# Seven products of half sums in place of eight for part of a decoder's input projection, on one Trainium2 core

## The reference, cut to what matters

```
xn = rmsnorm(x, norm_gain)
h  = xn @ w_in                                   # 1024 -> 5960 columns
cb, cc, cu, cz, q, k, v, az, iq, ik, iw, gc, ga = split_cols(h)
y_conv = cb * short_conv(cc * cu) * silu(cz)                       # width 512
y_attn = sparse attention(q, k, v; top 256 keys by iq, ik, iw) * silu(az)
m = sigmoid(gc) * (y_conv @ w_up_conv) + sigmoid(ga) * (y_attn @ w_up_attn)
x = x + m @ w_out ; y = rmsnorm(x, final_gain)
```

## Time and profile before

| | us |
|---|---|
| median of 3 runs | 2862.32 (2861.93 to 2862.68) |
| profiled execution, own time | 2864.7 |
| its span | 2862.9 |
| prompt tiles, from normalising tile 1 (T = 2) to the end of the stage | 213.8 to 1833.5 |
| sample stage | 1838.9 to 2357.9 |

### The profile page before, as it was taken

One profiled execution on the slowest core, in us unless ns is written; L12 is line 12 of the kernel. 1 busy time (PEld: TensorE's weight loads), 2 busy tenths in 40 slices (PEclk: granted clock), 3 DMA queues, 4 the chain that ended last, 5 costly groups with the idle time before them and its releaser, 6 DMA issues. The chain is left out here.

```text
span 2862.9 us, 31303 instructions
## 1 busy us (share of the span) xinstructions
PE 2663.6 (93%) x11650; PEld 1481.7 (52%) x11650; DVE 1932.3 (67%) x3938; ACT 832.8 (29%) x1363; POOL 49.0 (2%) x65
## 2 busy tenths in 40 slices
PE   7987998999999999999999998899999868999988
PEld 5743444454444545454545454555555546676653
DVE  5219899987797989887989997126995014454443
ACT  4222233322323233333333333311221342231210
POOL 0000000000000000000000000100000100000000
PEclk9998999999999999999999999899999989999999
DMA  7111111111111111111111010131225749453307
GB/s 213 32 37 35 43 42 41 31 46 35 40 45 35 36 38 30 41 38 37 33 35 35 26 43 24 52 115 72 103 104 126 220 193 292 156 187 108 129 30 30
DMA packets 212680, 215.33 MB, mean 75 GB/s; under 512 B 76720, under 2 KB 199216, under 8 KB 208880
## 3 DMA queue, kind: packets, MB, share of 16 engines
q1 hardware_dynamic: 203824, 153.13, 18.6%
q0 software_dynamic: 7072, 60.18, 6.8%
q10 hardware_dynamic: 1632, 0.01, 0.1%
HBM read 157.56 MB, written 55.72 MB: 74 GB/s over the span
## 5 line engine op out<-in xcount | busy, mean ns | idle before, releaser
L787 PE MATMUL attn_ps_r<-xnT,early 128*128 128x424 f32 (+2 forms) x2464 | 993.1, 543 | 30.5 <-ACT early L638 15.7
L115 DVE TENSOR_SCALAR_CACHE_REDUCE early<-early 128x384 uint8<-128x384 f32 (+13 forms) x462 | 681.8, 1476 | 11.5
L787 PEld LDWEIGHTS attn_ps_r<-xnT,early 128*128 128x128 f32 x2464 | 442.9, 191 | 441.0 <-issue 423.5
L1089 PE MATMUL samp_ps_r<-xnT,early 128*128 128x424 f32 (+1 forms) x800 | 288.2, 523 | 6.1 <-PEq L89 6.1
L657 ACT ACTIVATE attn_probT<-attn_ps_p 128x512 f32<-128x512 f32 (+1 forms) x288 | 151.9, 571 | 407.2 <-PE attn_ps_p L832 407.0
L1646 PE MATMUL merge_ps_y<-merge_w_out,merge_merged 128*128 128x512 f32 (+1 forms) x544 | 235.0, 592 | 1.2 <-DVE merge_merged L1775 1.2
L1089 PEld LDWEIGHTS samp_ps_r<-xnT,early 128*128 128x128 f32 x800 | 153.2, 192 | 138.9 <-issue 138.3
L715 DVE SCALAR_TENSOR_TENSOR early<-attn_relu,early 128x512 f32<-128x512 f32 (+3 forms) x266 | 182.1, 684 | 31.4 <-ACT attn_relu L674 4.1
L638 ACT ACTIVATE early<-attn_ps_r 128x424 f32<-128x424 f32 (+1 forms) x130 | 67.9, 523 | 427.8 <-PE attn_ps_r L787 426.5
L817 PE MATMUL attn_ps_s<-kT,qT 64*128 64x512 f32 (+3 forms) x640 | 163.9, 592 | 25.6 <-DVE early L744 18.5
L832 PE MATMUL attn_ps_p<-ident,prob 128*128 128x128 f32 x1088 | 156.8, 283 | 25.8 <-ACT prob L693 25.8
(11 more groups left out here) (231 smaller groups left out, 2366.0 us busy)
## 6 DMA issues: line engine op xcount, KB each, us to landing
rest_t<-early SPq DMA_DIRECT2D x144, 212.0 KB, 1.9
early<-in_w_in SPq DMA_DIRECT2D x104, 256.0 KB, 3.4
early<-in_x_prompt SPq DMA_DIRECT2D x16, 512.0 KB, 4.0
merge_x<-in_x_prompt SPq DMA_DIRECT2D x8, 1024.0 KB, 5.0
out_y_prompt<-merge_y POOLq DMA_DIRECT2D x16, 512.0 KB, 4.1
rest_t<-early SPq DMA_DIRECT2D x36, 208.0 KB, 2.1
merge_ga<-rest_t SPq DMA_DIRECT2D x7, 1024.0 KB, 10.9
merge_gc<-rest_t SPq DMA_DIRECT2D x7, 1024.0 KB, 9.4
```

What stands on the lines that cost most here:

```text
L115: self.v.done(self.nc.vector.tensor_scalar(self.hits, self.x, limit, None, op, ALU.add, accum_out=self.count))
L787: ins = nc.tensor.matmul(ps_r[:, 0:width], w_rest[:, n % 2, k, :], c.xnT[:, k, t0:t0 + width], start=(k == 0), stop=(k == KC - 1))
L1089: ins = nc.tensor.matmul(ps_r[:, i % 2, 0:width], w_rest[:, (slot0 + j) % 2, k, :], c.xnT[:, k, t0:t0 + width], start=(k == 0), stop=(k == ...
```

## The change

The tokens are now cut in two parts. The sample tokens moved to the front of `xnT` (columns 0 to 63), and the prompt tokens follow.

**Plain part.** The first 832 columns (64 sample and 768 prompt tokens) of every block are computed as before, in two items of 416 columns and eight matmuls ("whole" items). All 36 blocks have this part in tiles 3 to 11, two blocks ("a pair", four items) at a time: 1, 1, 2, 1, 3, 2, 3, 2, 3 pairs.

**Parts.** For the other 1280 tokens, two blocks (2 x 128 columns of weights), two halves of the width (2 x 512) and two sets of 320 tokens form a 2 x 2 by 2 x 2 block product. Seven products of sums replace the eight plain ones (the Strassen-Winograd form). One such "group" is seven items ("parts") of four matmuls with 320 columns each; there are 18 pairs times 2 sets = 36 groups. 18 groups run in tiles 12 to 15 (4, 4, 5, 5), and 18 in the sample stage.

- POOL makes the four sums of weights of each pair in SBUF after the pair's plain part (128 x 512 each, 72 in all, L803 to L809) and writes them to `sums` in HBM (L812).
- POOL makes four sums of tokens (128 x 4 x 320) for each of the two slabs of tokens (L819).
- Some products accumulate onto the one before in PSUM; ACT copies each item out, and POOL adds pairs of copies, three adds of 128 x 320 per group (L822 and, in the sample stage, L1333). The copies lie in `xnT` (columns no longer needed) and in `rest`.
- ACT's copy of a product waits until the store of the same result of the group before has landed, and the copy of product 1 waits for POOL's second add of its own group.
- Weights go into eight places of 128 x 512 (four near, four in the tail of `prob`; from tile 12 on only the four near ones) instead of two of 128 x 1024.
- In slots of tiles with parts, `shares` rounds to whole items.
- In the sample stage, the write of `bias_scratch` and the copies back moved from POOL's queue to SP's, at fixed places among the rest products: the wait for the search stands before product 102 of 126, the first copies before product 107. The last two copies and the merge stage's first loads follow the last store. The gather into `xnT` now waits for all stores of the groups.

```diff
+PAIRS_OF_TILE = [0, 0, 0, 1, 1, 2, 1, 3, 2, 3, 2, 3, 0, 0, 0, 0, 0, 0]
+GROUPS_OF_TILE = [0, 0, 0, 0, 0, 0, 0, 0, 0, 0, 0, 0, 4, 4, 5, 5, 0, 0]
+ORDER1 = (3, 5, 0, 2, 4, 6, 1)
+ORDER2 = (0, 3, 2, 5, 4, 1, 6)
+OPENS = (0, 1, 3)
...
+def operands_of(c, group):
+    b11, b12, b21, b22 = tokens_of(c, group)
+    t1, t2, t3, t4 = sums_of(c)
+    return [b11, b21, t2, t1, t3, b22, t4]
...
 # AttentionPlan.shares
+        if any(item.kind == "part" for item in self.items[T]):
+            edges = [min(ends, key=lambda end: abs(end - edge)) for edge in edges]
...
 # prompt stage, POOL
+                def sum_weights(pair, n, load):
+                    a11, a12, a21, a22 = parts = [places[plan.place[load + x]] for x in range(4)]
+                    pool.wait_ge(rest_done, n + 1)
+                    nc.gpsimd.tensor_tensor(a22, a21, a22, ALU.add).then_inc(w_summed, 1)
...
+                    for x in range(4):
+                        pool.dma_start(a["sums"][pair][:, x], parts[x]).then_inc(w_sums_out[pair % 2], 16)
+                def difference(x, out, left, right, group):
...
+                    nc.gpsimd.tensor_tensor(out, left, right, ALU.subtract).then_inc(halved, 1)
+                def add(i, j):
+                    nc.gpsimd.tensor_tensor(result_of(c, i), result_of(c, i), result_of(c, j), ALU.add).then_inc(added, 1)
...
 # prompt stage, PE
+                            if k == 0 and n:
+                                pe.wait_ge(rest_kept, n)
+                            if k % 4 == 0:
+                                pe.wait_ge(w_in[plan.place[load]], 32 * (plan.turn[load] + 1))
...
+                                ins = nc.tensor.matmul(ps_r[:, 0:HALF], w, operands_of(c, item.of)[item.i][:, k, :],
+                                                       start=(k == 0 and item.i in OPENS), stop=(k == 3),
...
 # sample stage, SP
+                for n in range(in_all):
+                    g, at = GROUP0 + n // 7, n % 7
+                    if n == in_all - 24:
+                        sp.wait_ge(biased, 1)
+                        sp.dma_start(a["bias_scratch"].rearrange("b t k -> (b t) k"), score[0:ST, :]).then_inc(bias_out, 16)
+                    if n == in_all - 19:
+                        sp.wait_ge(bias_out, 16)
+                        replicate(0)
+                        replicate(1)
+                    sp.wait_ge(rest_done, n + 1)
+                    load(n + RING)
...
+                    if at == 6:
+                        sp.wait_ge(r_added, 3 * (g - GROUP0) + 3)
+                        store(g, 0)
...
 # sample stage, POOL
+                combine(GROUP0, RESTS[0])
                 pool.wait_ge(i_turned, 4 * DB)
                 keys(0)
...
-                pool.wait_ge(rest_done, len(steps))
+                combine(RESTS[2], RESTS[3])
+                pool.wait_ge(rest_done, in_all)
+                for s in range(4):
+                    pool.wait_ge(group_stored[s], 16 * len(groups))
                 keys(2)
                 values(1)
...
 # sample stage, ACT
+                        if i not in (1, 3, 5):
+                            act.wait_ge(group_stored[i // 2], 16 * g)
+                        elif i == 1:
+                            act.wait_ge(r_added, 3 * g + 2)
```

More of the change, by code:

```diff
@@ L164, in stage_norm, with product_pieces @@
+def product_pieces(a, group, i, dst):
+    if isinstance(WEIGHTS[i], tuple):
+        block, half = WEIGHTS[i]
+        return weight_pieces(a, 2 * (group % NPAIR) + block, half, dst)
+    src = a["sums"][group % NPAIR][:, WEIGHTS[i]]
+    return [(dst[:, 2 * n:2 * n + 2], src[:, 2 * n:2 * n + 2]) for n in range(2)]
 def stage_norm(nc, c, a):
@@ L214, in xnT_of @@
         def xnT_of(t):
-            return c.xnT[:, :, t * P:t * P + rows(t)]
+            return c.xnT[:, :, ST + t * P:ST + (t + 1) * P] if t < NT else c.xsT
         def at(t):
@@ new lines, in __init__ @@
+        self.order = [item for items in self.items for item in items]
+        self.loads += [("part", GROUP0 + n // 7, ORDER2[n % 7], 0) for n in range(RING)]
+        users, taken, ends = {}, [0] * RING, {}
+        for n, item in enumerate(self.order):
+            for load in range(item.load, item.load + item.steps // 4):
+                ends[load] = n
+            if item.kind == "whole":
+                first = item.load - 2 * (item.of % 2)
+                ends.update({load: n + 2 for load in range(first, first + 4)})
@@ new lines, in __init__ @@
+        self.place, self.turn, self.after, place, latest = [], [], [], -1, -1
+        near = next(item.load for item in self.order if item.kind == "part")
+        own = len(self.loads) - RING
+        for load in range(len(self.loads)):
+            if load >= own:
+                place = load - own
+            else:
+                place = (place + 1) % (RING if load < near else 4)
+            latest = max(latest, ends.get(users.get(place), -1))
+            if load >= own + 4:
+                latest = len(self.order) - 1
+            self.place.append(place)
+            self.turn.append(taken[place])
+            self.after.append(latest)
+            users[place] = load
+            taken[place] += 1
@@ L479, in __init__ @@
         self.weighs0 = before([G * len(x) for x in self.subs])
-        self.stores0 = before([sum(load[0] == "rest" for _, load, _ in x) for x in self.items])
         self.fill = [self.shares(T) for T in tiles]
@@ L1845, in stage_tokens @@
         c.xnT = sb("xnT", [P, KC, S + ST])
-        c.xsT = c.xnT[:, :, S:S + ST]
+        c.xsT = c.xnT[:, :, 0:ST]
+        c.w_far = [c.xnT[:, 0:4, PASS1 + n * P:PASS1 + (n + 1) * P] for n in range(4)]
         c.qs = sb("qs", [P, 2, 4, ST])
```

477 lines of the change are left out of this document (316 added, 161 removed).

## The result

The changed kernel took 3066.39 us (median of 4 runs, 3062.53 to 3072.14) against 2862.12 us before: ratio 1.0715, 95% interval 1.0694 to 1.0736, so some 7% slower. The forecast was 2887 us, 0.9% slower; 204 us came where 25 were expected, far outside the range. The profiled execution's span is 3070.4 us against 2862.9.

What follows compares the result with a forecast made beforehand. DVE was taken to bound the prompt tiles' shrinking, PE the sample stage. Terms -8 + 12 + 1 in the first part and +19 in the sample stage gave +24: 2889 profiled, 2887 us median; range 2850 and a little below to 2924.

Steps and rivals of the forecast that it cites:

- DVE's floor: Prompt tiles: a tile shrinks only by DVE's slack; tiles 12 to 15 by 27 us, DVE's waits there.
- the price of pairs: Tiles 3 to 11: a pair's plain part costs PE 22.4 us, a block 28.43; tile 5 grows by 14 us.
- PE could be 51 us shorter ... -27: Tiles 12 to 15: PE's work falls by 51 us net, but DVE's waits cap the gain at 27 us.
- POOL beside DVE: Prompt tiles: POOL's new sums, adds and differences slow DVE by 0 to 44 us, taken as +12.
- Start of the sample stage: PE waits for ACT's copy, which needs POOL's second add behind its masks: +11 us.
- Sample stage, PE's work ... -17.3: 126 products of 2.15 us take PE 270.9 us, where ten blocks took 288.2: -17.3 us.
- SP's wait for the search: Sample stage: SP stands 13.5 us before product 102 for the search, holding loads and stores behind it: +10 us.
- Copies beside stores: Sample stage: a store issued behind the copies for the heads lands late and holds ACT's copy of product 112: +10 us.
- End: After the products: third gather waits for all stores and shares engines with copies and merge loads, +4; exponentials among fewer copies, +1.
- POOL takes DVE's time: Rival, chance 0.15: POOL's work costs DVE 44 us in place of 12 in tiles DVE bounds, giving 2919 us.
- the faster rival: Rival, chance 0.25: the sample stage's stalls don't reach PE, giving 2850 us.
- The rival of starved weights: Rival: four near places of half a weight block starve PE from tile 12 on, 5 us more; no separate chance given.

Runs made afterwards that it cites:

- The experiment on the kernel before: Kernel before the change, with the rest's matmuls of tiles 12 to 15 only half as wide: 2835.69 us (ratio 0.9908).
- the edit: Changed kernel, with SP storing the last two plain items before it waits for the sums of weights: 3059.44 us (ratio 1.0682).
- the mended and regrouped kernel: Changed kernel with two sets of whole-row places, mended queue orders and waits, one pair moved from tile 5 to 2, one group from 14 to 16: 2937.74 us.

## Why the prediction was wrong, step by step

- **Right: tiles as buckets.** "DVE's floor" and the price of pairs: tile 5 +17 (forecast +14), tiles 7 and 9 +11 and +10 (+10.3), tile 8 -10 (-11.1). The experiment on the kernel before gave 27.7 us where the step said 27. Misses: tile 10 -3 (-11.1), and tiles 3, 4 and 6 together +4 (-4); with POOL idle these went to -7 and -4.
- **Wrong, 34 us: the step "PE could be 51 us shorter ... -27" in tiles 12 to 15.** They got 7.4 us longer. Tiles 12 and 13 gave 14 us together, where half the PE work in the kernel before gave 25; tile 14 with five groups was held by PE (+12), with 145.9 us of work and 18.7 idle, most of it short waits for ACT's exponentials and copies (rows below); tile 15 carried POOL's differences (+9.7; 6.2 went with POOL idle). I capped the sum of four tiles by the sum of their waits, where each tile has its own bound. PE's waits in tile 14, after:

```profile
PE attn_ps_p L1093 <- ACT prob L944: 8.1, 7, 2.4
PE attn_ps_r L1043 <- ACT xnT L888: 4.2, 8, 0.5
```

- **Missed: SP's queue in tile 11**, tile +31 where +10 was forecast; the edit took 11 of it back. The new wait for the sums stood in the diff, and I didn't ask what is queued behind it.
- **POOL beside DVE: the mechanism was right, the size low.** A sum of 512 columns took 1.26 us at the least and 1.32 to 1.50 on average by line, not 0.92; DVE's busy time grew by 44 us, which was the upper end, and some 19 to 24 us reached the end where +12 was taken.
- **Start of the sample stage:** the wait at POOL's masks came as forecast (PE waited 9.07 us for it, forecast 11), but the stage's start grew by 38.8: three waits behind stores add 14.5, and the 28 products took 71.5 us of PE at a granted clock of 0.85, where 60 would be 28 x 2.15. The wait for the barrier grew by 2.7 where +1 was taken.
- **The step that failed most: "Sample stage, PE's work ... -17.3".** It took seven products in a row as 7 x 2.15 us and costed stores only where copies stand before them. But every store's place is needed again one group (15 us) later, and for result 0 two products later. PE waited 92.7 us for ACT in 17 places; the forecast had some 30 there. And the price of 2.15 us held only without waits: the 126 products took 304.5 us of PE, not 270.9, so the term of -17.3 came out at +16.5; some 29 of these 34 us are the lower granted clock, an estimate from the clock during the products. The rows for the stores were at hand: in the earlier trace rows late stores already held ACT, 15.0 us in two waits.
- **"SP's wait for the search" didn't exist.** With PE that late, the search was done at 2287.1 and SP wrote it at 2319.1, 32 us after: it delayed the copies that DVE needs (DVE waited 69.1 us for them, 22.9 before), not PE's loads. "Copies beside stores" did come: 30.9 us in one wait, forecast 10.
- **End:** +30.9 where +4 was taken. The forecast named both causes, the gather behind the stores and the copies that share the engines with it, but bounded them by waits of a kernel in which the copies stand behind the gather on its own queue. Beside it, on SP's, they took PE's wait from 8.3 to 44.9 us.
- **DMA as a whole wasn't costed.** A product of 2.15 us needs 256 KB of weights, where a block of 28.4 us needed 512 KB.
- **Slips in the sums, without weight here.** 18 groups at 28 x 0.538 are 271.3 us, not 272.2, and half to one and a half of two stalls of 10 us gives 2877 to 2897, not 2868 to 2905.

The rivals: "POOL takes DVE's time" was right on DVE and explains 19 to 24 us; the faster rival fell. The rival of starved weights came true in another place: from tile 12 on PE waits for no load, but in tiles 4 to 11 it waits once per tile for a pair's weights, 22 us in all, where it waited for none before.

What stays open is the mended and regrouped kernel, some 74 us over before. In the profiled executions it is 69, of which 37 are in the prompt tiles (20 in tile 11), 23 between these and the index scores, and 9 in the products. By the experiment that idled POOL, in the unmended kernel, up to 24 are POOL's; the waits for weights stayed; the rest wasn't taken apart. No version tried beat the kernel before.

## What to carry to other kernels

Fewer multiplications paid only where PE bounded the stretch, and there the smaller products brought more weights, stores and copies per microsecond: cost the bytes, and how soon each place is needed again, before counting the matmuls. A cap by an engine's slack holds tile by tile, not for a sum of tiles. Which queue a transfer stands on decides whom it delays, even if it moves the same bytes. And take the price of a matmul from a stretch with waits like those that will come, not from one without.

## What the runs showed of the hardware

A short wait can cost PE more than its length. Windows after, around one store wait (length, busy PE, PEld, DVE, ACT, POOL, granted clock):

```profile
2150.66:2154.66 4.00, 0.01 (x2) 0.03 (x1) 3.99 (x1) 0.58 (x2) 0.00 (x0) 0.98 0.96 176
2154.66:2158.49 3.83, 3.83 (x9) 2.54 (x10) 3.73 (x5) 0.18 (x1) 0.00 (x0) 0.58 0.29 51
2158.49:2167.10 8.61, 8.61 (x33) 6.08 (x32) 8.40 (x9) 1.75 (x4) 2.58 (x3) 1.00 0.46 113
2167.10:2171.57 4.47, 4.47 (x17) 2.85 (x15) 4.37 (x5) 0.44 (x1) 0.00 (x0) 1.00 0.82 156
2171.57:2174.41 2.84, 0.00 (x1) 0.03 (x1) 2.84 (x1) 0.58 (x2) 0.00 (x0) 1.00 1.07 227
2174.41:2178.30 3.89, 3.89 (x9) 2.50 (x10) 3.78 (x5) 0.19 (x1) 0.00 (x0) 0.57 0.39 51
```

After PE stood idle for 4.00 and for 2.84 us, the product that followed ran at a granted clock of 0.58 and 0.57, near the lower level (1.2 of 2.4 GHz), and took 3.83 and 3.89 us where the next four took 8.61 / 4 = 2.15. So each of these two waits cost about 1.7 us on top. Not every wait did: behind one of 2.75 us the product at 2214.03 ran at 1.00 and took 2.23 us, while behind one of 2.73 us the product at 1989.98 ran at 0.59 and took 3.75. Over all 17 waits the first products behind them took some 22 us more than 2.15 us each. With two sets of places, where most of the waits are gone, the same products took 19 us less.
